# The head of a two-block transformer kernel: x loaded and normalised first, the first shift columns summed on TensorE and VectorE

## The reference

```python
c_act = jax.nn.silu(c)
mod = c_act @ ada_w[layer] + ada_b[layer]
sh1, sc1, g1, sh2, sc2, g2 = jnp.split(mod, 6, axis=-1)
h = modulate(rms_norm(x, norm_g[layer, 0]), sh1, sc1)    # y * (1 + scale) + shift
y = gmlp_mixer(h, a_w_in[layer], ...)                    # z = gelu(h @ w_in), ...
```

## Time and profile before

| | us |
|---|---|
| median of 3 runs | 1561.31 (1560.72 to 1562.01) |
| the profiled execution, its own time | 1560.54 |
| its span (first to last instruction) | 1558.8 |
| TensorE busy | 1511.9 (97%) |
| VectorE busy | 1096.1 (70%) |
| ScalarE busy | 692.4 (44%) |
| GpSimd busy | 286.6 (18%) |

### The profile page before, as it was taken

The page is one execution under the profiler, slowest core; times in us unless marked ns, Lnnn a source line. Parts: engine busy times, 40 slices in busy tenths (PEclk is TensorE's granted clock), DMA queues, the critical chain, the costliest instruction groups (busy, mean ns, idle before and its releaser), DMA issues.

```text
span 1558.8 us, 20890 instructions
## 1 busy us (share of the span) xinstructions
PE 1511.9 (97%) x8187; PEld 1255.4 (81%) x8187; DVE 1096.1 (70%) x1607; ACT 692.4 (44%) x1177; POOL 286.6 (18%) x230
## 2 busy tenths in 40 slices
PE   4999999999999999989999999999999999999998
PEld 3888888888888898977888988888888988677677
DVE  6798688889888754269884785556644815888775
ACT  3433551323214544357774541413233525877651
POOL 0200013223222000058870020011100011000210
PEclk9999999999999999999999999999999999999999
DMA  9774257578584215220001264433323133111101
GB/s 332 243 271 169 82 206 246 191 249 282 187 303 161 92 33 189 82 87 2 2 2 55 66 228 145 169 135 134 116 102 106 61 108 100 63 54 55 55 1 54
DMA packets 108808, 203.35 MB, mean 130 GB/s; under 512 B 6041, under 2 KB 13478, under 8 KB 108710
## 3 DMA queue, kind: packets, MB, share of 16 engines
q1 hardware_dynamic: 108710, 202.01, 37.9%
HBM read 199.90 MB, written 2.10 MB: 130 GB/s over the span
## 4 chain that ended last, share of the span: by engine, by line
PE 81%; DVE 10%; ACT 2%; DMA 2%; issue 2%; SPq 1%; POOL 1%; DVEq 0%; ACTq 0%
PE PS L2142 47%; PE PS L2095 19%; DVE MACC L1287 3%; PE PS L2474 3%; PE PS L2501 2%; PE PS L2464 2%; DVE WL L1253 2%; PE PS L2651 1%; PE PS L2404 1%; PE PS L2166 1%; DMA MRAW<-in_ada_w_dram 1%; POOL MROW L494 1%; DMA X<-in_x_dram 1%; PE PS L2673 1%; ACT SQ L755 1%
## 5 line engine op out<-in xcount | busy, mean ns | idle before, releaser
L733 ACT ACTIVATE WH<-RAW 128x2048 fp32r<-128x2048 f32 (+1 forms) x111 | 208.1, 1886 | 362.9 <-DMA RAW<-in_ff_w_in_dram 222.9
L1253 DVE TENSOR_TENSOR WL<-RAW,WH 128x2048 fp32r<-128x2048 f32 (+1 forms) x107 | 269.1, 2538 | 126.4 <-ACT WH L733 126.3
L494 POOL PARTITION_ALL_REDUCE MROW<-MACC x26 | 123.3, 4744 | 603.6 <-DVE MACC L1287 515.2
L2142 PE MATMUL PS<-WH,HIDh 128*128 128x512 f32 (+1 forms) x576 | 217.4, 378 | 0.0
L2142 PE MATMUL PS<-WH,HIDl 128*128 128x512 f32 (+1 forms) x576 | 217.3, 377 | 0.0
L2142 PE MATMUL PS<-WL,HIDh 128*128 128x512 f32 (+1 forms) x576 | 217.3, 377 | 0.0
L2142 PE MATMUL PS<-HTh,WH 128*128 128x512 f32 (+1 forms) x520 | 202.5, 389 | 0.7 <-DVE WL L1253 0.7
L2142 PE MATMUL PS<-HTl,WH 128*128 128x512 f32 (+1 forms) x520 | 202.4, 389 | 0.0
L2142 PE MATMUL PS<-HTh,WL 128*128 128x512 f32 (+1 forms) x520 | 202.3, 389 | 0.0
L1287 DVE SCALAR_TENSOR_TENSOR MACC<-MRAW,CS,MACC 128x512 f32<-128x512 f32 x168 | 126.3, 752 | 8.5 <-DMA MRAW<-in_ada_w_dram 1.0
L2095 PE MATMUL PS<-HTh,WH 128*128 128x256 f32 (+1 forms) x384 | 125.2, 326 | 6.8 <-DVE WL L1253 4.4
(11 more groups left out here) (344 smaller groups left out, 2977.1 us busy)
## 6 DMA issues: line engine op xcount, KB each, us to landing
MRAW<-in_ada_w_dram SPq DMA_DIRECT2D x44, 1024.0 KB, 7.4
RAW<-in_ff_w_in_dram SPq DMA_DIRECT2D x32, 1024.0 KB, 5.4
RAW<-in_ff_w_out_dram SPq DMA_DIRECT2D x32, 1024.0 KB, 5.1
RAW<-in_w_in_dram SPq DMA_DIRECT2D x16, 1024.0 KB, 5.2
MRAW<-in_w_ada_dram SPq DMA_DIRECT2D x12, 1024.0 KB, 8.7
RAW<-in_a_w_in_dram SPq DMA_DIRECT2D x8, 1024.0 KB, 9.7
MRAW<-in_kv_ada_w_dram SPq DMA_DIRECT2D x8, 1024.0 KB, 6.1
RAW<-in_kv_w_dram SPq DMA_DIRECT2D x6, 1024.0 KB, 5.4
```

The lines of the kernel that those rows point to most:

```text
L494: pool.partition_all_reduce(MROW[:], MACC[:], P, RADD).then_inc(m_red, 1)
L733: act.activation(WH[:, wslot(u), 0:width(u)], RAW[:, u % 4, 0:width(u)], ACT.Copy).then_inc(w_hi, 1)
L1253: dve.tensor_tensor(WL[:, u % 4, 0:width(u)], RAW[:, u % 4, 0:width(u)], WH[:, wslot(u), 0:width(u)].bitcast(F32), ALU.subtract).then_inc( ...
L2142: mm = pe.matmul(po, a, b_, start=(k == 0 and i == 0), stop=(k == KT - 1 and i == len(ops) - 1), skip_group_check=len(ops) > 3)
```

## The change

x is loaded right behind `PR1`, ahead of chunk 2. VectorE normalises the four tiles of x before it adds up anything, and TensorE turns them before it turns `PR0` and `PR2`. Of chunk 0, VectorE adds up only parts 4, 5 and 6. TensorE takes parts 0 to 3 and 7 itself (`shift_products`: the part's 128x128 piece as weights, the column k of silu(c) as the one moving column), adding up in four columns of PSUM bank 6, onto which `column(1)` adds VectorE's share. SyncE's loads of chunk 1 into `M3a` and `M3b` now wait for `m_red` to be 2, that is for `column(1)`.

```diff
--- before.py
+++ after.py
@@ -365,6 +365,8 @@
         rows(PR1, C_NG2, as_rows(norm_g_2[0]))
         rows(PR1, C_LNG, as_rows(a_ln_g[0]))
         rows(PR1, C_B1, cmp_b1.rearrange("j (r p) -> (j r) p", p=P))
+        for tt in range(TT):
+            load_x(tt)
         mod(0, 2)
         rows(PR0, B_L[0], ada_b.rearrange("l (r p) -> (l r) p", p=P))
         rows(PR0, B_KV, as_rows(kv_ada_b))
@@ -381,19 +383,17 @@
 
             for h in range(2):
                 if freed:
-                    sp.wait_ge(m_acc, freed + 4 * h)
+                    sp.wait_ge(m_red, freed)
                 sp.dma_start(M3[h][:], cols_of(ada[0], 512 * chunk)[:, 4 * h:4 * h + 4, :]).then_inc(m3_in[h], 16)
             n.mod += 1
 
         first_mod(0)
-        for tt in range(TT):
-            load_x(tt)
         half_weight(a_w_in[0], D, 0)
         sp.dma_start(WSR[:], a_w_s[0].rearrange("g t s -> t g s")).then_inc(ws_in, 16)
         sp.dma_start(LNB[:], a_ln_b.to_broadcast([P, D])).then_inc(ln_in, 16)
         half_weight(a_w_in[0], D + 512, 2)
         mod(0, 3)
-        first_mod(1, 12)
+        first_mod(1, 2)
         half_weight(a_w_in[0], D, 1)
         half_weight(a_w_in[0], D + 512, 3)
         n.chunk = 2
@@ -1267,7 +1267,7 @@
             lo(2 * n.chunk + 2)
             lo(2 * n.chunk + 3)
 
-        def mod_acc(vec, acc=MACC[:], after=None, part=range(KT), raw=None, m=None):
+        def mod_acc(vec, acc=MACC[:], after=None, part=range(KT), raw=None, m=None, begin=0):
 
             m = n.mod if m is None else m
             if after is None and m >= 1:
@@ -1280,10 +1280,10 @@
                 elif k % 4 == 0:
                     dve.wait_ge(m_in[k // 4], 16 * (m - 1) if m >= 4 else 8 * m + 16)
                 src = MRAW[:, k // 4, k % 4, :] if raw is None else raw[k // 4][:, k % 4, :]
-                if k == 0:
-                    dve.tensor_scalar(acc, src, vec[:, 0:1], None, ALU.mult).then_inc(m_acc, 1)
+                if k == begin:
+                    dve.tensor_scalar(acc, src, vec[:, k:k + 1], None, ALU.mult).then_inc(m_acc, 1)
                 else:
-                    dve.wait_ge(m_acc, 8 * m + k)
+                    dve.wait_ge(m_acc, 8 * m + k - begin)
                     dve.scalar_tensor_tensor(out=acc, in0=src, scalar=vec[:, k:k + 1], in1=acc,
                                              op0=ALU.mult, op1=ALU.add).then_inc(m_acc, 1)
 
@@ -1356,7 +1356,7 @@
                 dve.tensor_scalar(V[:, tt, :], X[:, tt, :], ST[:, 2, tt:tt + 1], None, ALU.mult).then_inc(n_xn, 1)
 
             def column(i, ch):
-                src = PS[:, 4 if i < 2 else 3, 256 + 4 * i:260 + 4 * i]
+                src = PS[:, (4, 6, 3, 3)[i], 256 + 4 * i:260 + 4 * i]
                 dve.wait_ge(m_red, i + 1)
                 dve.tensor_copy(MCOL[:, 4 * ch:4 * ch + 4], src).then_inc(m_post, 1)
                 dve.sem_inc(m_c, 1)
@@ -1364,23 +1364,23 @@
 
             dve.wait_ge(full, 1)
             dve.tensor_copy(C1[:], PS[:, 4, 0:PAR1]).then_inc(cols, 1)
+            for tt in range(TT):
+                normed(tt)
+            jobs[0] += TT
             dve.wait_ge(act_c, 1)
             mod_acc(CS)
-            dve.wait_ge(full, 4)
+            dve.wait_ge(full, 8)
             dve.tensor_copy(C02[:], PS[:, 5, 0:P + PAR2]).then_inc(ev_d, 1)
             dve.wait_ge(ev_d, 1)
             dve.sem_inc(ev_d, 1)
-            mod_acc(CS, MROW[:], 0, range(4), M3, 1)
+            mod_acc(CS, MROW[:], 0, range(4, 7), M3, 1, begin=4)
+            dve.wait_ge(m_acc, 11)
+            for _ in range(5):
+                dve.sem_inc(m_acc, 1)
             column(0, 2)
-            mod_acc(CS, MROW[:], 0, range(4, KT), M3, 1)
-            normed(0)
-            normed(1)
             column(1, 0)
             dve.wait_ge(m_post, 2)
             coefs(0, AB, 8, 0, C_NG, slice(0, 4)).then_inc(coef0, 1)
-            normed(2)
-            normed(3)
-            jobs[0] += TT
             lo_half(0, 0).then_inc(w_first, 1)
             for k in range(4):
                 if k == 2:
@@ -2239,18 +2239,22 @@
         pe.wait_ge(pool_c, 3)
         pe.wait_ge(par1_in, 16 * 7)
         pe.transpose(PS[:, 4, 0:PAR1], PR1[:], IDENT[0:PAR1, 0:PAR1]).then_inc(full, 1)
-        pe.wait_ge(par_in, 16 * 11)
-        pe.transpose(PS[:, 5, 0:P], PR0[:], IDENT[:])
-        pe.transpose(PS[:, 5, P:P + PAR2], PR2[:], IDENT[0:PAR2, 0:PAR2]).then_inc(full, 3)
-
         def column(i, acc):
 
             pe.wait_ge(m_acc, 8 * i + 8)
             for b in range(4):
                 o = 256 + 4 * i + b
-                mm = pe.matmul(PS[:, 4 if i < 2 else 3, o:o + 1], acc[:, P * b:P * b + P], ONES[:], start=True,
-                               stop=True)
+                mm = pe.matmul(PS[:, (4, 6, 3, 3)[i], o:o + 1], acc[:, P * b:P * b + P], ONES[:], start=(i != 1),
+                               stop=True, skip_group_check=(i == 1))
             mm.then_inc(m_red, 1)
+
+        def shift_products(part):
+
+            for k in part:
+                pe.wait_ge(m3_in[k // 4], 16)
+                for b in range(4):
+                    pe.matmul(PS[:, 6, 260 + b:261 + b], M3[k // 4][:, k % 4, P * b:P * b + P], CS[:, k:k + 1],
+                              start=(k == 0 and b == 0), stop=False, skip_group_check=True)
 
         def turn_x(tt, half):
 
@@ -2265,12 +2269,18 @@
 
         pe.wait_ge(ones_c, 1)
         pe.wait_ge(cols, 1)
-        column(0, MACC)
-        pe.wait_ge(m_post, 1)
-        column(1, MROW)
         for tt in range(TT):
             turn_x(tt, 0)
         xn[0] += TT
+        pe.wait_ge(par_in, 16 * 11)
+        pe.transpose(PS[:, 5, 0:P], PR0[:], IDENT[:])
+        pe.transpose(PS[:, 5, P:P + PAR2], PR2[:], IDENT[0:PAR2, 0:PAR2]).then_inc(full, 3)
+
+        pe.wait_ge(act_c, 1)
+        shift_products(range(4))
+        column(0, MACC)
+        shift_products(range(7, KT))
+        column(1, MROW)
 
         def first_part(c_, k):
 
```

## The result

| | before | after |
|---|---|---|
| median of 10 runs | 1561.57 us (1560.24 to 1562.46) | 1565.73 us (1561.49 to 1566.93) |
| ratio, 95% interval | | 1.0021 (1.0012 to 1.0031) |
| the profiled execution: time, span | 1560.54, 1558.8 | 1565.82, 1564.1 |

The forecast was 1565.9. A second set of the changed kernel, beside the experiments, gave 1565.84 against 1562.28, a ratio of 1.0022 (1.0011 to 1.0032).

The account below looks back on a forecast made before the run. The start of TensorE's first large product was taken to bound the kernel; M3a at 20.7, the 11.8 us stream and the hand-over put it at 35.8, not 31.22. So 1561.31 + 4.6 = 1565.9 us, range 1560.9 to 1567.9.

Parts of the forecast that it names:

- What bounds the kernel: The start of TensorE's first large product, 31.22 us; the rest was to move with it nearly whole.
- x first: Head DMA stream: x's four tiles put M3a off by 5.2 us to 20.7; the x work itself costs nothing.
- The stream: TensorE from 20.7: seven groups of one-column products at 1.69 each, low clock, 11.8 us plus 0.15, done at 32.65.
- Hand-over: From the stream's end to the first large product: coefs done at 33.4, WL at 34.6, product at 35.8.
- The new wait on SyncE: Chunk 1's loads wait until 32.7 instead of 26.22; costed at nothing, covered by queued loads landing until 37.2.
- The size: Whole kernel: first large product at 35.8 instead of 31.22, so +4.6 us and a median of 1565.9.
- Rival A: TensorE's clock rises during the one-column products: shift between -1.5 and +1.6, 1559.8 to 1562.9 us; chance 0.32.
- Rival B: Head: x off the chain gains a little; data order leaves WL ending near 30.1; chance 0.06, shared with anything else.
- Rival C: TensorE's one-column products do not overlap: 19.7 us instead of 11.8, total 1573.8; chance 0.04.

Follow-up runs that it names:

- The two halves: Against the kernel before: x first with all sums on VectorE, 1562.74 us; x late with the sums on TensorE, 1559.22 us; both against 1561.22.

## Why the prediction was right

- **What bounds the kernel.** The first large product came 4.76 later, and the whole at equal clock 4.5. That the rest moves with it nearly whole was right, though not that nothing takes it back. With the two profiles matched product by product, the changed kernel is 5.8 behind up to 470, then 4.9, since the wait of 0.66 that before has there is gone; the pause of 1.05 puts on 1.0 at 674, and another wait is 0.5 shorter at 681. The runs show the limit of that step, too: it holds for a shift of everything in the head. A TensorE that alone is quicker gains little, since VectorE's row of sums is right behind it (the wait of 1.04 above).
- **x first.** 5.2 us more for `M3a` was right: 15.5 + 5.2 = 20.7, measured 20.76; `M3b` 23.5 for 23.3. The first x tile landed at 7.05 and not 7.7, which changes nothing. The x work was over at 15.5 (forecast 16.1).
- **The stream.** Seven groups from 20.89 to 32.99, 12.1 us for 11.8 + 0.15. That the level of the clock is its price, which I had read from two rows at 1.69 and 0.80, the run with the clock raised ahead shows inside one stream: 0.89 and 1.7. The high-level price in a stream is a little more than my 0.80.
- **Hand-over.** `coefs` ended at 33.64 (33.4), `WL` at 34.78 (34.6), the product at 35.98 (35.8).
- **The new wait on SyncE.** `M3a` for chunk 1 went out at 33.00 and landed 7.1 later, at 40.1, for 39.9 before; the DMA engines stayed full (386 GB/s from 36 to 41). Free, as costed.
- **The size.** The sum of +4.6 stands against +4.5 and +4.4 at equal clock, and +4.2 between the medians. In the profiled run the clock rose 2 us later behind the first large product than before, for which I had added nothing, and this cost 1.0 at the landmark (59.03 - 53.26 = 5.77, of which 4.76 is the shift). Of the 5.77 the spans show 5.3 at the end: the waits above leave it at 5.3 by 676, then before loses 1.6 in a fall of the clock at 676, which the changed kernel does not have, and the changed kernel loses 1.7 in one at 1475, which before does not have. So the mechanism was right, but that the number came out so close is in part luck: the later rise of the clock put on 1.0 that I had not counted, and later waits that I had not looked at gave some of it back.
- **Rival A** fell: in 12 us of one-column products, in both profiled runs of the changed kernel, the clock did not rise, and it fell when it had been up. Three of ten runs were at 1561.5 to 1562.4, which looks like A; their granted clock was 0.998 or 0.999, where before has 1559.4 and 1557.7 on average, 1.8 and 3.5 below its median. So the later falls tell most of it. For the two at 0.999 the distance is the full 4.6; but the one at 0.998, and one at 0.998 in the second set (1561.49 and 1561.10), are only 2.1 and 1.7 above before at that clock. No profile of such a run was taken, so that A never happens is not shown. **Rival B's** floor was about right: with two parts on TensorE the first large product was at 31.42, and no version with x first came ahead of 31.22. **Rival C** fell with the 1.705 a group.
- **What the forecast didn't have.** I priced the change as one path. The two halves apart are +1.9 and +0.1: the transposes of x, taken from right ahead of the large products to 11 us, had no price in my sum, but in the run that has them behind the stream the products that follow start at the high level.

## What to carry to other kernels

A product with one moving column cost here what one with 128 columns cost: at the high level 32 such instructions took 3.57 us (0.112 each) and 20 instructions of the 128-column fillers 2.23 (0.112 each), and a float32 product is two of them. In every profile here without fillers TensorE ran at the low level ahead of its first dense work. So price such sums at the level that rows ahead of the first dense work show, and compare them with the few VectorE instructions they replace (here 1.7 us on TensorE for 0.79 on VectorE). Moving an input ahead in a full DMA stream puts all behind it off by its own time (5.2 us here); the gain is there only if what it passes is not next on the path. In a head of a few tens of microseconds the engine just behind the critical one decides what a repair is worth: at the landmark, filling TensorE with the select out of the way gave 0.3 us until VectorE's copy was moved, and 1.6 with it. And a shift is followed to the end before it is called whole: a wait hundreds of microseconds later gave back 0.9 of it.

## What the runs showed of the hardware

- A stream of one-column products that keeps TensorE 100% busy by the profile neither raised the clock in 12 us nor held it: in two runs with fillers ahead it went from 1.00 to 0.50, some 3.7 us into the stream, and with one 128-column product to every four narrow ones 5.9 us into it. The Trainium skill, "TensorE: Matmul & The Clock Gate", the HAM clock gate, counts the warm-up in time of sustained activity and not in products; read plainly, this trace does not agree, since 12.1 us of such products without a gap did not raise the clock.
- Sixteen back-to-back transposes of 128 columns, behind such a stream, were followed by the high level: 27.58 to 31.23, the granted clock recorded from 31.4 on, and the next product, at 32.80, lasting 0.47. The same stream with nothing behind it left the clock low. The Trainium skill, on the same page under PE-mode transpose, says that the high level does not engage for transposes; here it came behind them. Transposes without the stream ahead of them were not run.
- The granted clock reads 1.00 before its first recorded change. For the head the durations have to tell the level: 0.63 and 0.40 for the same product.
